# Two y buffers and two x buffers in place of one and three, and fewer unconditional rounds, in the expert stage of a hybrid encoder layer

## The chip, the cores and the metric

The kernel runs on one core of a Trainium2 chip. The metric is the device time of one execution in microseconds; three executions of the kernel before are given, and one of them was profiled.

## The reference, cut to what matters

One layer over 1024 prompt rows and 64 sample rows of width 1024: modulated RMSNorm, an input projection, two kinds of attention, an output projection, then a mixture of experts, and a last RMSNorm. The change touches only the mixture of experts:

```python
def hier_moe(h, w_rg, b_rg, w_re, b_re, w_gate, w_up, w_down):
    ...                                   # top-1 of 4 groups, top-2 of the 8 experts in it
    combine = jnp.einsum('tke,tk->te', jax.nn.one_hot(expert_id, N_EXPERTS, dtype=jnp.float32), e_w)

    def expert_step(acc, args):
        wg, wu, wd, cw = args
        hh = jax.nn.silu(x @ wg) * (x @ wu)
        return acc + (hh * cw[:, None].astype(hh.dtype)) @ wd, None
```

There are 32 experts with a hidden width of 256. Each of the 1088 rows goes to two of them, so 2176 pairs of row and expert are computed. All of it is in float32.

## The kernel before

Five stages follow one another: modulation and norm of the input, projection with attention (to about 690 us), output projection with routing (to about 920 us), the experts, and the last norm. The routing stage writes a list in HBM: for each expert the rows that chose it, where each result goes, and its weight. The expert stage is the function `experts` (line 1442).

The work is cut into blocks of 64 rows of one expert, and a step computes two blocks at once, block A in partitions 0 to 63 and block B in 64 to 127. For these inputs there are 26 steps, numbered p = 0 to 25 here, in 13 rounds of two. The number of rounds n is data: each engine reads it from a table, and the program is written out for 17 rounds (34 steps). `in_rounds` (line 1478) writes the loop out. The first `SURE` = 9 rounds are always needed and stand without a branch, the others behind `If(n > u)`. `following` (line 1491) does the same for work that belongs to a later step.

Weights come from HBM. Block A's expert is one of at most three held in slots (`a_gu`, `a_dn`), 3 MB loaded by SyncE when a slot comes free, 10 times in all. Block B's weights are loaded anew in each step by ScalarE's queue, `b_gu` (2 MB, three buffers, issued at line 1503 after the silu three steps ahead) and `b_dn` (1 MB, two buffers, line 1505, after the y eviction two steps ahead).

One step p goes through these places:

- POOL reads a piece of the list into `entry` (line 1545, `listing`), gathers 128 rows of `h2` by it into `x[p % 3]` (line 1550, `gather`), and at the end scatters the result rows `y` to HBM (line 1572). All three are indirect DMAs of POOL's one queue. Rows of padding in a block are skipped.
- PE transposes the gathered rows (line 1584), multiplies them by gate and up weights (lines 1595 and 1598: 16 pairs of matmul records a step), transposes the gated hidden rows (line 1605), and multiplies by the down weights (lines 1618 and 1621: 8 pairs).
- ACT and DVE each move a half of the transposed rows (1671, 1737), make the gated hidden rows (silu at 1677, product at 1741), move the transposed hidden rows (1749), and evict a half of the result, times the routing weight, into `y` (1695 and 1754).

The order within the engines is written out by hand. PE does in body p: gate and up of p+1, the hidden transposes of p, the row transposes of p+2, down of p. ACT does: load of gate and up weights for p+3, its half of the rows of p+2, its half of y of p, load of down weights for p+2, silu of p+1. POOL does: the gather for p+4 (once the row transposes of p+1 are done and their buffer is free), the scatter of p (once both halves of y are written), the list read for p+7. There is one buffer `y`, so both evictions of step p wait until the scatter of step p-1 has landed. Before the loop POOL has issued three list reads, three gathers, three list reads, a gather and a list read.

Of the kernel before, what the change touches and what calls it, by code (L numbers as in the profile page):

```python
# [18 lines left out]
F32 = mybir.dt.float32  # L19
F32R = mybir.dt.float32r  # L20
I32 = mybir.dt.int32
ALU = mybir.AluOpType
ACT = mybir.ActivationFunctionType
# [24 lines left out]
STEPS = 2 * ROUNDS  # L48
SURE = (2 * TOK // P + 1) // 2
LOOK = STEPS  # L50
# [91 lines left out]
def build(nc, a, o):  # L142
    with ExitStack() as ctx:
# [24 lines left out]
        with ExitStack() as c:  # L168
# [5 lines left out]
                done=route.sb("done", [P, 2, 2 * NE]), steps=route.sb("steps", [P, 1]), cols=route.sb("cols", [P, 8]),  # L174
                x=[route.sb(f"x{j}", [P, D]) for j in range(3)])
            with ExitStack() as c2:
# [843 lines left out]
def mix_out(nc, s, a, o, k, g2):  # L1020
# [112 lines left out]
    def _(pool):  # L1133
        pool.memset(half[:, :], -0.5).then_inc(half_set, 1)
        pool.memset(entry[:, :, :], 0).then_inc(zeroed, 1)
        pool.memset(before[:, :], 0.0).then_inc(zeroed, 1)
        for j in range(3):
            pool.memset(route["x"][j][:, :], 0.0).then_inc(x_zeroed, 1)
# [27 lines left out]
        pool.wait_ge(listed, 32 * (NT + 1))  # L1166
        pool.wait_ge(x_zeroed, 3)

# [273 lines left out]
def experts(nc, s, a, k):  # L1442
# [11 lines left out]
    hT = s.sb("hT", [P, 2, P])  # L1454
    y = s.sb("y", [P, D])
    rank, first, held = (s.sb(n, [P, 2 * NE]) for n in ("rank", "first", "held"))
# [7 lines left out]
    listed = [s.sem(f"listed{j}") for j in range(4)]  # L1464
    gathered, scattered = [s.sem(f"gathered{j}") for j in range(3)], s.sem("scattered")
    gu_ld, dn_ld = [s.sem(f"gu_ld{j}") for j in range(3)], [s.sem(f"dn_ld{j}") for j in range(2)]
# [12 lines left out]
    def in_rounds(eng, n, body):  # L1479
        for u in range(ROUNDS):  # L1480
            if u < SURE:
                body(2 * u, n)
                body(2 * u + 1, n)
            else:
                with eng.If(n > u):
                    body(2 * u, n)
                    body(2 * u + 1, n)
                with eng.Else():
                    eng.nop()

    def following(eng, p, n, do):

        if p // 2 < SURE:
            do()
        elif p < STEPS:
            with eng.If(n > p // 2):
                do()
            with eng.Else():
                eng.nop()
# [43 lines left out]
    def _(pool):  # L1543
# [4 lines left out]
        def gather(p):  # L1548
            pool.wait_ge(listed[p % 4], 16 * (p // 4 + 1))
            pool.indirect_dma_start(x[p % 3][:, :], None, k["h2"], bass.IndirectOffsetOnAxis(ap=entry[:, p, 0:1], axis=0),  # L1550
                                    bounds_check=TOK - 1, oob_is_err=False).then_inc(gathered[p % 3], 16)

        for p in range(3):
            listing(p)
        for p in range(3):
            gather(p)
        for p in range(3, 6):
            listing(p)
        n = look(pool, T_ROUNDS, 0, 1, ROUNDS)

        def gather_ahead(p):
            pool.wait_ge(xT_ready, p - 2)
            gather(p)

        gather_ahead(3)
        listing(6)

        def body(p, n):
            following(pool, p + 4, n, lambda: gather_ahead(p + 4))
            pool.wait_ge(y_out_act, p + 1)  # L1570
            pool.wait_ge(y_out_dve, p + 1)
            pool.indirect_dma_start(k["yrows"], bass.IndirectOffsetOnAxis(ap=entry[:, p, 1:2], axis=0), y[:, :], None,  # L1572
                                    bounds_check=2 * TOK - 1, oob_is_err=False).then_inc(scattered, 16)
            following(pool, p + 7, n, lambda: listing(p + 7))

        in_rounds(pool, n, body)
        alone(pool, scattered, 32 * n, waited)

    @block.tensor
    def _(pe):  # L1580
        def transpose_x(p):
            pe.wait_ge(gathered[p % 3], 16 * (p // 3 + 1))
            for c in range(NC):
                ins = pe.transpose(xT_ps[:, c, :], x[p % 3][:, c * P:(c + 1) * P], ident)
            ins.then_inc(xT_ready, 1)
# [49 lines left out]
        def body(p, n):  # L1635
# [4 lines left out]
            elif p + 1 < STEPS:  # L1640
                if p // 2 + 1 < SURE:
                    gate_up(p + 1)
                    transpose_hidden(p)
                    transpose_x(p + 2)
                else:
                    with pe.If(n > p // 2 + 1):
                        gate_up(p + 1)
                        transpose_hidden(p)
                        transpose_x(p + 2)
                    with pe.Else():  # L1650
                        transpose_hidden(p)
            else:
                transpose_hidden(p)
# [5 lines left out]
    def _(act):  # L1659
# [29 lines left out]
        def body(p, n):  # L1689
            following(act, p + 3, n, lambda: load_gu(p + 3, expert(p + 3)))  # L1690
            following(act, p + 2, n, lambda: move_xT(p + 2))
            act.wait_ge(y_ready, p + 1)
            if p:
                act.wait_ge(scattered, 16 * p)
            act.activation(y[:, 0:512], y_ps[:, 0:512], ACT.Copy, scale=entry[:, p, 2:3].bitcast(F32))\
               .then_inc(y_out_act, 1)
# [9 lines left out]
    def _(dve):  # L1706
# [40 lines left out]
        def body(p, n):  # L1747
# [3 lines left out]
            dve.wait_ge(y_ready, p + 1)  # L1751
            if p:
                dve.wait_ge(scattered, 16 * p)
            dve.tensor_scalar(y[:, 512:1024], y_ps[:, 512:1024], entry[:, p, 2:3].bitcast(F32), None, ALU.mult)\  # L1754
               .then_inc(y_out_dve, 1)
# [183 lines left out]
```

## Time and profile before

| | us |
|---|---|
| median of three executions | 1355.49 |
| lowest, highest | 1351.79, 1362.63 |
| the profiled execution | 1351.79 |
| its span, first to last instruction | 1349.6 |
| expert stage in it, about | 926 to 1294 |
| PE busy | 1161.5 (86%) |
| mean granted TensorE clock | 0.941 of full speed |

Times in rows are microseconds from the start of the span unless marked ns. An "issue" or a "q" behind an engine's name (PEldq, ACTq) is its instruction queue, PEld is TensorE's weight load. A wait is put down to what came last before the instruction started.

### The profile page before, as it was taken

To read this page: it belongs to the slowest core of one execution; us is meant where nothing else is said; L and a number is where in the kernel's file an instruction comes from. 1 tells how busy PE (TensorE), PEld (TensorE's weight loads), DVE (VectorE), ACT (ScalarE), POOL (GpSimd) and SP (SyncE) were. 2 spreads that over 40 slices of the span, in tenths; PEclk is the share of its full clock that TensorE was granted. 3 is DMA by queue.
4 is the path that set the end of the run, shared out by engine and by line. 5 is a ranking of instruction groups with operands and counts; after the bars stand their busy time and mean duration, and the time that the engine had idled before them with its cause. 6 is when DMAs were issued, how large, how long until landed. Compare 5 with 4: busy or idle time off the path is not lost. (4 is left out here: it accounts for less than half of the span.)

```text
span 1349.6 us, 19893 instructions
## 1 busy us (share of the span) xinstructions
PE 1161.5 (86%) x7175; PEld 767.0 (57%) x7175; DVE 518.6 (38%) x1320; ACT 342.2 (25%) x854; POOL 295.1 (22%) x233
## 2 busy tenths in 40 slices
PE   4688999999999999999886999951998999899846
PEld 2346888888888888888773555521333333333312
DVE  2432244444444444535533466653112121111118
ACT  4422233333332333333442222110101011111102
POOL 2031313030302121110002565533112221211001
PEclk9677999999999999999998999975999899999978
DMA  9771202020102121110130111115998999999646
GB/s 372 291 287 50 71 19 89 1 88 3 60 11 70 53 78 45 54 53 26 47 140 8 63 53 57 47 32 236 419 393 313 386 379 388 376 374 363 249 185 250
DMA packets 53538, 218.56 MB, mean 162 GB/s; under 512 B 9904, under 2 KB 26680, under 8 KB 42560
## 3 DMA queue, kind: packets, MB, share of 16 engines
q1 hardware_dynamic: 36912, 117.26, 23.7%
q10 hardware_dynamic: 7632, 82.05, 15.3%
q0 software_dynamic: 8896, 17.93, 3.4%
q8 instruction: 63, 1.03, 0.3%
q14 instruction: 35, 0.29, 0.1%
HBM read 196.62 MB, written 30.03 MB: 168 GB/s over the span
## 5 line engine op out<-in xcount | busy, mean ns | idle before, releaser
L729 PE MATMUL att_piece_ps<-hT_hi,w_hi 128*128 128x384 f32 (+1 forms) x528 | 185.2, 351 | 2.0 <-DVE att_k_lo_sb L857 0.8
L1595 PE MATMUL moe_gu_ps<-moe_a_gu_sb,moe_xT_sb 128*64 x416 | 184.4, 596 | 2.0 <-DVE moe_xT_sb L1737 2.0
L1598 PE MATMUL moe_gu_ps<-moe_b_gu_sb,moe_xT_sb 128*64 128x512 f32 x416 | 184.4, 596 | 0.0
L729 PE MATMUL att_piece_ps<-hT_hi,w_lo 128*128 128x384 f32 (+1 forms) x528 | 173.6, 329 | 0.0
L729 PE MATMUL att_piece_ps<-hT_lo,w_hi 128*128 128x384 f32 (+1 forms) x528 | 173.2, 328 | 0.0
L916 DVE COPY att_pT_sb<-att_pT_ps 128x512 f32<-128x512 f32 (+2 forms) x192 | 94.6, 521 | 134.0 <-PE att_pT_ps L790 133.4
L1200 PE MATMUL mix_y_ps<-mix_w_out_sb,mix_oT_sb 128*128 128x512 f32 (+1 forms) x288 | 127.2, 600 | 2.2 <-ACT mix_oT_sb L1268 2.2
L1595 PEld LDWEIGHTS moe_gu_ps<-moe_a_gu_sb,moe_xT_sb 128*64 128x64 f32 x416 | 57.2, 138 | 121.2 <-issue 121.2
L977 ACT ACTIVATE att_probs_sb<-att_probs_sb,att_nmax_sb 128x640 f32<-128x640 f32 (+5 forms) x144 | 101.2, 703 | 42.1 <-DVE att_nmax_sb L902 41.3
L902 DVE CUSTOM_DVE_ANT_0 att_probs_sb<-att_s_ps,att_bias_sb 128x640 f32<-128x640 f32 (+5 forms) x144 | 95.2, 662 | 26.8 <-PE att_s_ps L778 14.6
L729 PEld LDWEIGHTS att_piece_ps<-hT_hi,w_hi 128*128 128x128 f32 x528 | 99.8, 189 | 9.4 <-issue 4.7
L992 ACT ACTIVATE keep_rows_all_sb<-att_o_ps,att_rden_sb 128x64 f32<-128x64 f32 x144 | 37.2, 309 | 261.0 <-PE att_o_ps L811 261.0
L706 POOL CAST w_hi<-att_w_raw_sb 128x1024 fp32r<-128x1024 f32 x21 | 21.8, 1038 | 364.8 <-PE att_piece_ps L729 331.7
L1618 PE MATMUL moe_y_ps<-moe_a_dn_sb,moe_hT_sb 128*64 x208 | 99.2, 621 | 1.5 <-DVE moe_hT_sb L1749 0.7
L729 PEld LDWEIGHTS att_piece_ps<-hT_lo,w_hi 128*128 128x128 f32 x528 | 100.0, 189 | 0.0
L729 PEld LDWEIGHTS att_piece_ps<-hT_hi,w_lo 128*128 128x128 f32 x528 | 99.7, 189 | 0.0
L1621 PE MATMUL moe_y_ps<-moe_b_dn_sb,moe_hT_sb 128*64 128x512 f32 x208 | 99.2, 621 | 0.0
L1754 DVE TENSOR_SCALAR moe_y_sb<-moe_y_ps,moe_entries_sb 128x512 f32<-128x512 f32 x26 | 19.5, 751 | 204.2 <-DMA expert_rows<-moe_y_sb,moe_entries_sb 193.5
L1200 PEld LDWEIGHTS mix_y_ps<-mix_w_out_sb,mix_oT_sb 128*128 128x128 f32 (+1 forms) x288 | 52.9, 186 | 69.9 <-issue 67.0
L790 PE MATMUL att_pT_ps<-keep_consts_sb,att_probs_sb 128*128 128x128 f32 (+2 forms) x560 | 87.6, 278 | 1.8 <-ACT att_probs_sb L977 1.7
L1572 POOL DMA_INDIRECT expert_rows<-moe_y_sb,moe_entries_sb x26 | 26.2, 1010 | 254.0 <-DVE moe_y_sb L1754 254.0
L805 PE MATMUL att_o_ps<-att_pT_sb,att_v_rows_sb 128*64 128x128 f32 (+1 forms) x1088 | 74.4, 277 | 7.7 <-DVE att_pT_sb L916 6.5
(280 smaller groups left out, 1801.6 us busy)
## 6 DMA issues: line engine op xcount, KB each, us to landing
moe_b_gu_sb<-in_w_gu ACTq DMA_DIRECT2D x26, 2048.0 KB
moe_b_dn_sb<-in_w_dn ACTq DMA_DIRECT2D x26, 1024.0 KB
moe_a_gu_sb<-in_w_gu SPq DMA_DIRECT2D x10, 2048.0 KB
keep_rows_all_sb<-in_w_ada SPq DMA_DIRECT2D x8, 2048.0 KB, 12.2
att_w_raw_sb<-in_w_qkv SPq DMA_DIRECT2D x21, 512.0 KB, 3.3
moe_a_dn_sb<-in_w_dn SPq DMA_DIRECT2D x10, 1024.0 KB
in_w_ada_sb<-in_w_ada SPq DMA_DIRECT2D x4, 2048.0 KB, 11.5
in_x_sb<-in_x_prompt SPq DMA_DIRECT2D x8, 512.0 KB, 7.0
```

What stands on the lines that cost most here:

```text
L729: ins = pe.matmul(bank[:, 0:hi - lo], w[:, kind, kc, :], x[:, kc, lo:hi], start=(m == 0), stop=(m == 3 * NC - 1))
L790: ins = pe.transpose(pT_ps[e % 2][0:m, b - b0, 0:r], probs[h][0:r, b * P:b * P + m], ident[0:r, 0:r])
L805: ins = pe.matmul(o_ps[head, 0:r], v, pT[h][0:m, b, 0:r], start=(b == 0), stop=(b == len(kb) - 1))
L902: dve.tensor_tensor_reduce(probs[h][0:r, 0:wide], s_ps[h][0:r, 0:wide], bias, -SCALE, BIG, ALU.add, ALU.min, nmax[0:r, 2 * at + h:2 * at + ...
L916: ins = dve.tensor_copy(pT[h][:, b0:b1, :], pT_ps[e % 2][:, 0:b1 - b0, :])
L977: act.activation(probs[h][0:r, 0:wide], probs[h][0:r, 0:wide], ACT.Exp, bias=nmax[0:r, 2 * at + h:2 * at + h + 1], scale=-1.0, accum_out=d ...
L992: ins = act.activation(rows_all[0:r, t, first + HD * h:first + HD * h + HD], o_ps[0:r, P + HD * h:P + HD * h + HD], ACT.Copy, scale=rden[0 ...
L1200: ins = pe.matmul(y_ps[0:r, 512 * n:512 * n + 512], oT[:, c, 0:r], w_out[:, c, 512 * n:512 * n + 512], start=(c == 0), stop=(c == NC - 1))
L1595: pe.matmul(gu_ps[p % 2][LANE[0], :], xT[:, c, LANE[0]], a_gu[:, bass.ds(slot, 1), c, :].rearrange("p a n -> p (a n)"), start=(c == 0), st ...
L1598: ins = pe.matmul(gu_ps[p % 2][LANE[1], :], xT[:, c, LANE[1]], b_gu[p % 3][:, c, :], start=(c == 0), stop=(c == NC - 1))
L1618: pe.matmul(y_ps[LANE[0], half], hT[:, c, LANE[0]], a_dn[:, bass.ds(slot, 1), c, half].rearrange("p a n -> p (a n)"), start=(c == 0), stop ...
L1621: ins = pe.matmul(y_ps[LANE[1], half], hT[:, c, LANE[1]], b_dn[p % 2][:, c, half], start=(c == 0), stop=(c == 1))
```

## The change

It does three things, all for the expert stage.

1. `y` has two buffers, with a semaphore `scattered` for each. The evictions of step p wait for the scatter of step p-2.
2. The gathered rows `x` have two buffers in place of three. In body p POOL gathers for p+3. Before the loop it issues two list reads and two gathers, four more list reads, and then, once the first row transposes are done, the gather for step 2 and a seventh list read. The routing stage clears two x buffers in place of three. The bytes held in SBUF stay the same.
3. `SURE` is gone. Only round 0 is without a branch, in all engines; rounds 1 to 8 are now conditional as 9 and up were.

```diff
-SURE = (2 * TOK // P + 1) // 2
...
-                x=[route.sb(f"x{j}", [P, D]) for j in range(3)])
+                x=[route.sb(f"x{j}", [P, D]) for j in range(2)])
...
-        for j in range(3):
+        for j in range(2):
             pool.memset(route["x"][j][:, :], 0.0).then_inc(x_zeroed, 1)
...
-    y = s.sb("y", [P, D])
+    y = [s.sb(f"y{j}", [P, D]) for j in range(2)]
...
-    gathered, scattered = [s.sem(f"gathered{j}") for j in range(3)], s.sem("scattered")
+    gathered, scattered = ([s.sem(f"{n}{j}") for j in range(2)] for n in ("gathered", "scattered"))
...
     def in_rounds(eng, n, body):
         for u in range(ROUNDS):
-            if u < SURE:
-                body(2 * u, n)
-                body(2 * u + 1, n)
+            if u == 0:
+                body(0, n)
+                body(1, n)
...
     def following(eng, p, n, do):
-        if p // 2 < SURE:
+        if p // 2 == 0:
             do()
...
-        for p in range(3):
-            listing(p)
-        for p in range(3):
-            gather(p)
+        listing(0)
+        listing(1)
+        gather(0)
+        gather(1)
+        n = look(pool, T_ROUNDS, 0, 1, ROUNDS)
+        for p in range(2, 6):
+            following(pool, p, n, lambda: listing(p))
+
+        def third():
+            pool.wait_ge(xT_ready, 1)
+            gather(2)
+            following(pool, 6, n, lambda: listing(6))
+
+        following(pool, 2, n, third)
+
+        def gather_ahead(p):
+            pool.wait_ge(xT_ready, p - 1)
             gather(p)
-        for p in range(3, 6):
-            listing(p)
-        n = look(pool, T_ROUNDS, 0, 1, ROUNDS)
-
-        def gather_ahead(p):
-            pool.wait_ge(xT_ready, p - 2)
-            gather(p)
-
-        gather_ahead(3)
-        listing(6)
 
         def body(p, n):
-            following(pool, p + 4, n, lambda: gather_ahead(p + 4))
+            following(pool, p + 3, n, lambda: gather_ahead(p + 3))
             pool.wait_ge(y_out_act, p + 1)
             pool.wait_ge(y_out_dve, p + 1)
-            pool.indirect_dma_start(k["yrows"], bass.IndirectOffsetOnAxis(ap=entry[:, p, 1:2], axis=0), y[:, :], None,
-                                    bounds_check=2 * TOK - 1, oob_is_err=False).then_inc(scattered, 16)
+            pool.indirect_dma_start(k["yrows"], bass.IndirectOffsetOnAxis(ap=entry[:, p, 1:2], axis=0), y[p % 2][:, :], None,
+                                    bounds_check=2 * TOK - 1, oob_is_err=False).then_inc(scattered[p % 2], 16)
             following(pool, p + 7, n, lambda: listing(p + 7))
 
         in_rounds(pool, n, body)
-        alone(pool, scattered, 32 * n, waited)
+        alone(pool, scattered[0], 16 * n, waited)
+        alone(pool, scattered[1], 16 * n, waited)
...
-                if p // 2 + 1 < SURE:
+                with pe.If(n > p // 2 + 1):
                     gate_up(p + 1)
                     transpose_hidden(p)
                     transpose_x(p + 2)
-                else:
-                    with pe.If(n > p // 2 + 1):
-                        gate_up(p + 1)
-                        transpose_hidden(p)
-                        transpose_x(p + 2)
-                    with pe.Else():
-                        transpose_hidden(p)
+                with pe.Else():
+                    transpose_hidden(p)
...
             act.wait_ge(y_ready, p + 1)
-            if p:
-                act.wait_ge(scattered, 16 * p)
-            act.activation(y[:, 0:512], y_ps[:, 0:512], ACT.Copy, scale=entry[:, p, 2:3].bitcast(F32))\
+            if p >= 2:
+                act.wait_ge(scattered[p % 2], 16 * (p // 2))
+            act.activation(y[p % 2][:, 0:512], y_ps[:, 0:512], ACT.Copy, scale=entry[:, p, 2:3].bitcast(F32))\
                .then_inc(y_out_act, 1)
```

DVE's half of the eviction is changed as ACT's, and `gather` and `transpose_x` count their semaphores and buffers by two.

## Rows read from the trace of the kernel before

**Rows 1.** The page, part 2: busy tenths in 40 slices of 33.7 us.

```profile
PE   4688999999999999999886999951998999899846
...
DMA  9771202020102121110130111115998999999646
```

**Rows 2.** Windows: length, busy per engine, then clock, DMA share, GB/s.

```profile
950.00:962.00 12.00, 11.01 (x56) 4.13 (x54) 1.11 (x2) 0.98 (x2) 2.99 (x3) 1.00 1.01 420
...
926.00:1002.30 76.30, 55.42 (x262) 22.13 (x264) 10.07 (x23) 7.66 (x13) 16.03 (x16) 0.83 0.99 406
...
1002.30:1265.50 263.20, 241.87 (x1164) 91.55 (x1160) 45.77 (x80) 33.49 (x61) 56.69 (x57) 0.97 0.92 368
...
1265.50:1294.00 28.50, 19.88 (x94) 7.12 (x94) 5.48 (x10) 3.37 (x7) 3.83 (x4) 0.99 0.35 122
```

**Rows 3.** Waits, 920 to 1310: who waited for whom; total, times, longest us.

```profile
ACT moe_y_sb L1695 <- DMA expert_rows<-moe_y_sb,moe_entries_sb: 195.4, 23, 11.0
...
DVE moe_y_sb L1754 <- DMA expert_rows<-moe_y_sb,moe_entries_sb: 193.5, 23, 10.9
...
PE moe_hT_ps L1605 <- DVE moe_gate_sb L1741: 26.3, 17, 3.2
...
PE moe_xT_ps L1584 <- DMA route_x_sb<-h_rows,moe_entries_sb: 14.0, 1, 14.0
```

**Rows 4.** Tile moe_y_sb, 900 to 1310: the scatter, its time to landing.

```profile
DMA to landing us min/median/max: 3.2/11.4/17.9
```

**Rows 5.** Line 1545, 920 to 1310: the list reads, their time to landing.

```profile
DMA to landing us min/median/max: 5.9/10.8/18.5
```

**Rows 6.** Timeline of POOL: first gather; scatters of steps 2 and 22.

```profile
930.07 0.99 POOL L1550 DMA_INDIRECT route_x_sb<-h_rows,moe_entries_sb  x1 [3.00 <-DMA moe_entries_sb<-lists,route_at_sb]
...
1002.32 1.02 POOL L1572 DMA_INDIRECT expert_rows<-moe_y_sb,moe_entries_sb  x1 [9.43 <-DVE moe_y_sb L1754]
...
1265.45 0.99 POOL L1572 DMA_INDIRECT expert_rows<-moe_y_sb,moe_entries_sb  x1 [12.24 <-DVE moe_y_sb L1754]
```

**Rows 7.** Timeline, all engines, start of stage and two steady steps.

```profile
942.42 1.97 PE L1584 MATMUL moe_xT_ps<-keep_consts_sb,route_x_sb 128*128 128x128 f32 x8 [13.96 <-DMA route_x_sb<-h_rows,moe_entries_sb]
...
1121.27 0.69 ACT L1695 ACTIVATE moe_y_sb<-moe_y_ps,moe_entries_sb 128x512 f32<-128x512 f32 x1 [9.71 <-DMA expert_rows<-moe_y_sb,moe_entries_sb]
...
1122.90 1.02 POOL L1572 DMA_INDIRECT expert_rows<-moe_y_sb,moe_entries_sb  x1 [10.03 <-DVE moe_y_sb L1754]
...
1123.06 0.34 ACTq L1503 DMA_DIRECT2D moe_b_gu_sb<-in_w_gu  x1
...
1123.28 0.44 PE L1605 MATMUL moe_hT_ps<-keep_consts_sb,moe_gate_sb 128*128 128x128 f32 x2 [1.90 <-DVE moe_gate_sb L1741]
...
1124.52 0.64 PE L1618 MATMUL moe_y_ps<-moe_a_dn_sb,moe_hT_sb 128*64 x1
...
1125.55 0.99 POOL L1550 DMA_INDIRECT route_x_sb<-h_rows,moe_entries_sb  x1 [0.30 <-issue]
...
1128.01 0.59 PE L1595 MATMUL moe_gu_ps<-moe_a_gu_sb,moe_xT_sb 128*64 x1
...
1135.40 0.44 PE L1605 MATMUL moe_hT_ps<-keep_consts_sb,moe_gate_sb 128*128 128x128 f32 x2 [0.35 <-DVE moe_gate_sb L1741]
...
1136.64 0.64 PE L1618 MATMUL moe_y_ps<-moe_a_dn_sb,moe_hT_sb 128*64 x1
```

**Rows 8.** Lines 1496 and 1485: branches, ns; PE in a conditional round.

```profile
L1496 PEldq COMPARE_BRANCH  x9: 65/169/356, 1175.1 to 1273.5; - x9
...
L1485 PEldq COMPARE_BRANCH  x12: 65/169/5407, 1191.9 to 1295.1; - x12
...
1252.87 0.44 PE L1605 MATMUL moe_hT_ps<-keep_consts_sb,moe_gate_sb 128*128 128x128 f32 x2 [1.37 <-DVE moe_gate_sb L1741]
...
1254.21 0.64 PE L1618 MATMUL moe_y_ps<-moe_a_dn_sb,moe_hT_sb 128*64 x1
```

**Rows 9.** Line 1138: the memsets of the x buffers, ns.

```profile
L1138 POOL MEMSET route_x_sb<- x3: 967/967/967, 695.0 to 696.8; 128x1024 f32 x3
```

More of the change, by code:

```diff
@@ L1166, in _ @@
         pool.wait_ge(listed, 32 * (NT + 1))
-        pool.wait_ge(x_zeroed, 3)
+        pool.wait_ge(x_zeroed, 2)
     @block.tensor
@@ L1549, in gather @@
             pool.wait_ge(listed[p % 4], 16 * (p // 4 + 1))
-            pool.indirect_dma_start(x[p % 3][:, :], None, k["h2"], bass.IndirectOffsetOnAxis(ap=entry[:, p, 0:1], axis=0),
-                                    bounds_check=TOK - 1, oob_is_err=False).then_inc(gathered[p % 3], 16)
-        for p in range(3):
-            listing(p)
-        for p in range(3):
-            gather(p)
-        for p in range(3, 6):
-            listing(p)
-        n = look(pool, T_ROUNDS, 0, 1, ROUNDS)
-        def gather_ahead(p):
-            pool.wait_ge(xT_ready, p - 2)
-            gather(p)
-        gather_ahead(3)
-        listing(6)
+            pool.indirect_dma_start(x[p % 2][:, :], None, k["h2"], bass.IndirectOffsetOnAxis(ap=entry[:, p, 0:1], axis=0),
+                                    bounds_check=TOK - 1, oob_is_err=False).then_inc(gathered[p % 2], 16)
+        listing(0)
[12 more added lines that the diff above has]
+            pool.wait_ge(xT_ready, p - 1)
+            gather(p)
         def body(p, n):
-            following(pool, p + 4, n, lambda: gather_ahead(p + 4))
+            following(pool, p + 3, n, lambda: gather_ahead(p + 3))
             pool.wait_ge(y_out_act, p + 1)
             pool.wait_ge(y_out_dve, p + 1)
-            pool.indirect_dma_start(k["yrows"], bass.IndirectOffsetOnAxis(ap=entry[:, p, 1:2], axis=0), y[:, :], None,
-                                    bounds_check=2 * TOK - 1, oob_is_err=False).then_inc(scattered, 16)
+            pool.indirect_dma_start(k["yrows"], bass.IndirectOffsetOnAxis(ap=entry[:, p, 1:2], axis=0), y[p % 2][:, :], None,
+                                    bounds_check=2 * TOK - 1, oob_is_err=False).then_inc(scattered[p % 2], 16)
             following(pool, p + 7, n, lambda: listing(p + 7))
         in_rounds(pool, n, body)
-        alone(pool, scattered, 32 * n, waited)
+        alone(pool, scattered[0], 16 * n, waited)
+        alone(pool, scattered[1], 16 * n, waited)
     @block.tensor
@@ L1581, in transpose_x @@
         def transpose_x(p):
-            pe.wait_ge(gathered[p % 3], 16 * (p // 3 + 1))
+            pe.wait_ge(gathered[p % 2], 16 * (p // 2 + 1))
             for c in range(NC):
-                ins = pe.transpose(xT_ps[:, c, :], x[p % 3][:, c * P:(c + 1) * P], ident)
+                ins = pe.transpose(xT_ps[:, c, :], x[p % 2][:, c * P:(c + 1) * P], ident)
             ins.then_inc(xT_ready, 1)
@@ L1751, in body @@
             dve.wait_ge(y_ready, p + 1)
-            if p:
-                dve.wait_ge(scattered, 16 * p)
-            dve.tensor_scalar(y[:, 512:1024], y_ps[:, 512:1024], entry[:, p, 2:3].bitcast(F32), None, ALU.mult)\
+            if p >= 2:
+                dve.wait_ge(scattered[p % 2], 16 * (p // 2))
+            dve.tensor_scalar(y[p % 2][:, 512:1024], y_ps[:, 512:1024], entry[:, p, 2:3].bitcast(F32), None, ALU.mult)\
                .then_inc(y_out_dve, 1)
```

## The prediction

> **What bounds the kernel now.** I read four things in turn: the slices of the page, windows over the expert stage, the waits in it, and the timeline of two steps. The slices [rows 1] show where the change can act: PE is at 9 tenths nearly everywhere, and the DMA engines are busy only at the start and in slices 28 to 37, which are the expert stage (926 to 1294 us). Everything before 924 us is touched by one memset alone, so the whole sum is about this stage.
>
> The windows [rows 2] split it. From 926 to 1002 the DMA share is 0.99: three resident experts, the first streamed ones and the first rows all load at once, and steps 0 and 1 run in that. From 1002.3 to 1265.5 it is 0.92 at 368 GB/s with PE busy 241.87 of 263.2 us. The last 28.5 us have share 0.35. The middle window is chosen because the scatter of step 2 is issued at its start and that of step 22 at its end [rows 6]: (1265.45 - 1002.32) / 20 = 13.16 us a step. I call the length of a step T.
>
> The waits [rows 3] name a loop. ACT and DVE stand 195.4 and 193.5 us before their halves of the y eviction, 23 times, and what ends it is always the scatter of the step before, out of the same y buffer. Few of these microseconds are worth anything as such. PE's own stalls are what count: 26.3 us over 17 waits for the gated hidden rows (line 1741), which ACT and DVE can only make after the y eviction they are stuck in. PE waited for gathered rows once, at the very start (14.0 us), and never for weights: no weight tile stands among the releasers of its waits.
>
> The timeline [rows 7] shows one turn: y eviction 1121.27, the scatter issued 1122.90 (1.63 later), and it lands 11.4 us after its issue in the median [rows 4]. 1.63 + 11.4 = 13.0, the step of 13.16 almost exactly. So the middle stretch is bound by the round trip of the scatter.
>
> **Part one: two y buffers.** The eviction of step p now waits for scatter p-2. That allows 2T for a round trip of 13.0, so with T above 11 it is never last. The wait goes; three limits are next.
>
> PE itself: down starts are at 1124.52 and 1136.64, 12.12 apart, with 0.35 idle in between [rows 7], so a step of pure PE work is 11.77. Taken over the whole window it is 241.87 / 20 = 12.09 [rows 2], because the granted clock there was 0.97 of its upper level (2.4 GHz), with stretches at the lower one, and step starts don't overlap perfectly. T is at least 11.77 to 12.09.
>
> DMA: a share of 0.92 over 263.2 us is 242.1 us of work, 12.1 per step [rows 2]. Nothing in the change takes a byte away. T is at least 12.1, and that only with the DMA engines never idle. The window from 926 shows that 0.99 is possible when much is outstanding. Here the weights are fetched at most three steps ahead, each load released by the step's silu, so I take 0.97: 242.1 / 0.97 / 20 = 12.48, say 12.5. From both sides: 0.92 (nothing gained) gives 13.16, 1.0 gives 12.1.
>
> The Trainium skill, page "HBM Reference", section "Specifications (TRN2)", puts a core's effective share at about 358 GB/s and says that a core streaming alone measures about 425. By the first figure the stage, at 368, would be at its ceiling already and the sum would be zero; by the second there is room. The trace agrees with the second: 420 GB/s from 950 to 962 [rows 2].
>
> Loads that are released earlier: silu of step p no longer stands behind a late eviction, so the load of gate and up weights (issued at 1123.06, after silu [rows 7]) moves ahead relative to PE's work. That keeps the queue fuller and is why I dare 0.97. Gain of part one: 20 x (13.16 - 12.5) = 13.2 us.
>
> **Part two: two x buffers.** A gather is issued one step later: where POOL issued p+4 after the scatter of p-1 and a list read, it now issues p+3. The order on POOL is scatter, list read, gather, all in one queue; nothing else is queued behind them but the next scatter. The allowance: the y eviction of p-1 starts 3.6 us after its down (1124.52 to 1128.01 [rows 7], and 0.1 to start, an estimate), and the transposes of p+3 start 1.0 before the down of p+1 (the 1.24 us from 1123.28 to 1124.52 hold the two hidden transposes, then these), so it is 2T - 4.6. The gather is issued 1125.55 - 1121.27 = 4.3 after the eviction starts [rows 7]. It must land within 2T - 8.9 of its issue: 14.6 us at T = 11.77, 16.1 at T = 12.5.
>
> No view prints a gather's time to landing. From below: the scatter ahead of it in the queue lands 11.4 - 2.65 = 8.8 after the gather's issue, and a scatter alone takes 3.2 (the least of [rows 4]): 12.0. The first gather, with the DMA share at 0.99, took 942.42 - 930.07 = 12.4 [rows 6, 7]. From above: 18.5, the longest list read [rows 5], or 17.9, the longest scatter [rows 4]. I take 14 to 16, nearer the lower end where most rows are: just in time at T = 12.5. It costs nothing while PE has a step's work in hand; if that cover is gone, PE stands in the transposes (line 1584), the down product and the eviction behind them are late, and the loop gives T = (g + 8.9) / 2 for a mean landing g. It is worse than now only from g = 17.4 on.
>
> The start: the gather of step 2 moves from just after the second to behind the first transposes (end 944.4 [rows 7]). It has nearly two steps; late by at most 18.5 - 14.6 = 3.9 us, taken as 0, since the DMA engines are full there anyway and set the pace.
>
> **Part three: conditional rounds.** Rounds 1 to 8 (16 steps) now sit behind branches on PE, ACT, DVE and POOL, as rounds 9 to 12 do already. On PE such a branch took 0.17 us in the median [rows 8], issued ahead of its work. From hidden transposes to down it was 1.24 in an unconditional step [rows 7] and 1254.21 - 1252.87 = 1.34 in a conditional one [rows 8]: 0.1 x 16 = 1.6 us at most, 0 at least; I take 0.7.
>
> The Trainium skill, page "Runtime: NRT & Kernel Launch", section "Instruction fetch mechanics", says that a taken branch out of the two pages held makes the engine fetch before it goes on. By that rule each of the 8 rounds could stall; by the rows of the short jumps the part is worth the 0.7 just given.
>
> The memset that falls away (0.967 us of POOL at about 697 us [rows 9]) lies beside PE's work in the stage before and is worth 0 to 1; I take 0. The two waits at the end for the two scatter semaphores replace one, 0. Steps 0 to 2 and 23 to 25 gain nothing: the first are DMA bound (0.99), the last have a free queue (share 0.35) and PE does its chain.
>
> **The sum.** -13.2 + 0.7 = -12.5 us. The span of 1349.6 becomes 1337.1, the profiled execution's 1351.79 becomes 1339.3; the median of the three runs lies 3.7 above that execution, so 1355.5 - 12.5 = **1343.0**.
>
> **Rivals.**
> A, the full gain: T = 12.1, the bound of data and nearly that of PE. 20 x 1.06 = 21 us: 1334. For it: 0.99 has been reached, and clock dips vanish with the stalls (down to 11.77 by PE). Against: the loads are released by PE's own progress, and the three resident-expert loads come in bursts. The loosest edge, T = 11.77, would be 27.8 us, 1328.
> B, the gather takes the place: g about 16.9 while an expert load shares the engines, T = 12.9, gain 5, 1350. For it: landings of 17.9 and 18.5 occur [rows 4, 5]. Against: medians near 11.
> C, the other sign: PE waits in line 1584 for nearly every step. With g = 18.5, T = 13.7, +10.8; first gathers +3.9, branches +1.6: +16, 1371.5. It decides from a mean landing of 17.4. For it: the three transfers of a step stand in one queue, and with the engines fuller each takes longer. Against: a late gather also stops PE's releases of weight loads, and the queue clears.
> D, branches stall for a fetch: one branch of line 1485 took 5.407 us [rows 8], a far jump over the unused rounds. Eight such are +43: 1398. Against: all the near ones are of some 0.2 us. It is what the page "Runtime: NRT & Kernel Launch" of the Trainium skill would mean here.
> E, the data ceiling of 368 is real: no change, 1355. It is what the first figure of the page "HBM Reference" of the Trainium skill would mean here.
>
> **How the numbers follow.** Forecast (gain 8 to 17, 1338 to 1348) 0.40; A 0.17; B 0.24; C 0.13; D 0.03; E 0.03. One per cent, 13.6 us, is about what a measurement of this kernel can tell from nothing, and the forecast lies just inside it. Faster by over 1%: A and about half the forecast, 0.37. Within 1%: the other half, B, E, and the mild part of C, 0.49. Slower: 0.14. The range leaves out D, the worst half of C and the edge of A: 1330 to 1368; cases of both signs are in it.
>
> **What would show it.** Part one: the waits of lines 1695 and 1754 on the scatter gone, those on line 1621 in their place; PE's wait at line 1605 near 0. The data limit: DMA share near 0.97 between the scatters of steps 2 and 22, these 250 us apart. Part two: waits of line 1584 on the gather few and short; over 10 us in total is B, over 30 is C. Part three: no idle time of PE at round starts. The forecast is wrong if scatters still come 13 us apart with the share at 0.92, or closer than 12.

## The result

The changed kernel takes 1370.57 us in the median of eight executions (1362.44 to 1373.47) against 1357.45 of the kernel before on the same chip (1351.79 to 1362.63): a ratio of 1.0084, with a 95% interval of 1.0060 to 1.0108. It is slower by 11 us by the ratio, and by 13 by the two medians. The range of 1330 to 1368 did not hold it, and a gain had been forecast. A second set on another chip gave 1.0081 (1.0052 to 1.0110).

The profiled execution has a span of 1368.6 us against 1349.6. Where most of the 19 us are, the same windows show: length, then busy time with instruction count of PE, PE's weight load, DVE, ACT and POOL, then granted clock, DMA share and GB/s. The second one runs from the scatter of step 2 to that of step 22, as the window of before did.

```profile
926.00:1002.30 76.30, 53.69 (x254) 21.45 (x256) 12.10 (x34) 7.86 (x13) 18.64 (x19) 0.82 0.98 401
...
999.70:1279.30 279.60, 250.19 (x1164) 96.90 (x1162) 45.77 (x80) 33.41 (x61) 57.69 (x58) 0.94 0.88 351
```

Up to 1002 us nothing has changed much: share 0.98 for 0.99, PE busy 53.69 for 55.42 [rows 2]. Between the two scatters there are now 279.6 us in place of 263.1, a step of 13.98 for 13.16, and the DMA share is 0.88 where it was 0.92. That is 16.4 of the 19 us; the scatter of step 2 comes 2.6 us earlier than before, and what follows the scatter of step 22 takes 5.2 longer (1368.6 - 1279.3 against 1349.6 - 1265.5). The DMA engines, which were to be the new bound, stand idle more than before. PE's busy time has grown from 241.87 to 250.19 us for the same 1164 instructions, and its clock has gone from 0.97 to 0.94.

The waits from 920 to 1320 us (engine and line, what it waited for, total, times, longest), where [rows 3] showed the scatter:

```profile
PE moe_xT_ps L1588 <- DMA route_x_sb<-h_rows,moe_entries_sb: 45.8, 10, 14.0
...
ACT moe_y_sb L1694 <- PE moe_y_ps L1625: 99.0, 26, 9.8
...
PE moe_hT_ps L1609 <- DVE moe_gate_sb L1740: 1.5, 1, 1.5
```

The scatter no longer stands among what ACT waits for; it waits for the down product of PE, as it should. The stall of 26.3 us at the hidden rows is down to 1.5. In their place PE waits 45.8 us for gathered rows, ten times and not once. Without the first, 14.0 us long as before, that is 31.8 us: above the 30 at which the prediction had said "C".

The timeline of POOL, start and length first, shows the two scatters that give the step (1279.26 - 999.70, over 20), and one gather in between:

```profile
999.70 1.02 POOL L1575 DMA_INDIRECT expert_rows<-moe_y_sb,moe_entries_sb  x1 [8.88 <-DVE moe_y_sb L1753]
...
1055.23 0.99 POOL L1549 DMA_INDIRECT route_x_sb<-h_rows,moe_entries_sb  x1 [0.30 <-issue]
...
1279.26 1.01 POOL L1575 DMA_INDIRECT expert_rows<-moe_y_sb,moe_entries_sb  x1 [14.96 <-DVE moe_y_sb L1753]
```

### The profile page after: what moved, and what is told of

The parts are those of the page before. It is cut to its first block and busy times, and to the rows that moved or that the text cites. A ratio compares the mean times of both kernels' runs of the same rounds, so it can differ in the third digit from the quotient of the medians.

```text
span 1368.6 us, 20186 instructions
## 1 busy us (share of the span) xinstructions
PE 1169.7 (85%) x7175; PEld 772.9 (56%) x7175; DVE 519.8 (38%) x1320; ACT 342.2 (25%) x854; POOL 294.5 (22%) x232
## 5 line engine op out<-in xcount | busy, mean ns | idle before, releaser
L1199 PE MATMUL mix_y_ps<-mix_w_out_sb,mix_oT_sb 128*128 128x512 f32 (+1 forms) x288 | 130.3, 612 | 2.2 <-ACT mix_oT_sb L1267 2.2
L1622 PE MATMUL moe_y_ps<-moe_a_dn_sb,moe_hT_sb 128*64 x208 | 106.0, 657 | 1.8 <-issue 1.0
L1625 PE MATMUL moe_y_ps<-moe_b_dn_sb,moe_hT_sb 128*64 128x512 f32 x208 | 106.1, 658 | 0.0
L1575 POOL DMA_INDIRECT expert_rows<-moe_y_sb,moe_entries_sb x26 | 26.3, 1011 | 270.8 <-DVE moe_y_sb L1753 270.8
L1588 PE MATMUL moe_xT_ps<-keep_consts_sb,route_x_sb 128*128 128x128 f32 x208 | 33.2, 312 | 45.8 <-DMA route_x_sb<-h_rows,moe_entries_sb 45.8
## 6 DMA issues: line engine op xcount, KB each, us to landing
keep_rows_all_sb<-in_w_ada SPq DMA_DIRECT2D x8, 2048.0 KB, 12.1
moe_a_dn_sb<-in_w_dn SPq DMA_DIRECT2D x10, 1024.0 KB, 19.8
```

Of the source, the lines that this page charges most:

```text
L1199: ins = pe.matmul(y_ps[0:r, 512 * n:512 * n + 512], oT[:, c, 0:r], w_out[:, c, 512 * n:512 * n + 512], start=(c == 0), stop=(c == NC - 1))
L1622: pe.matmul(y_ps[LANE[0], half], hT[:, c, LANE[0]], a_dn[:, bass.ds(slot, 1), c, half].rearrange("p a n -> p (a n)"), start=(c == 0), stop ...
L1625: ins = pe.matmul(y_ps[LANE[1], half], hT[:, c, LANE[1]], b_dn[p % 2][:, c, half], start=(c == 0), stop=(c == 1))
```

## When the gather is late

The timelines of SyncE and PE of the changed kernel. The first three lines are SyncE issuing resident expert loads of 2 MB (the next line of code adds 1 MB), the others are PE, with the wait in front of an instruction in brackets:

```profile
998.86 0.34 SPq L1502 DMA_DIRECT2D moe_a_gu_sb<-in_w_gu  x1
...
1051.74 0.34 SPq L1502 DMA_DIRECT2D moe_a_gu_sb<-in_w_gu  x1
...
1249.41 0.34 SPq L1502 DMA_DIRECT2D moe_a_gu_sb<-in_w_gu  x1
...
1021.08 1.14 PE L1588 MATMUL moe_xT_ps<-keep_consts_sb,route_x_sb 128*128 128x128 f32 x8 [4.12 <-DMA route_x_sb<-h_rows,moe_entries_sb]
...
1074.26 1.97 PE L1588 MATMUL moe_xT_ps<-keep_consts_sb,route_x_sb 128*128 128x128 f32 x8 [4.42 <-DMA route_x_sb<-h_rows,moe_entries_sb]
...
1076.16 1.12 PE L1622 MATMUL moe_y_ps<-moe_a_dn_sb,moe_hT_sb 128*64 x1
...
1088.78 1.04 PE L1588 MATMUL moe_xT_ps<-keep_consts_sb,route_x_sb 128*128 128x128 f32 x8
...
1271.43 1.97 PE L1588 MATMUL moe_xT_ps<-keep_consts_sb,route_x_sb 128*128 128x128 f32 x8 [3.92 <-DMA route_x_sb<-h_rows,moe_entries_sb]
```

Seven expert loads are issued after the start, and seven gathers are late by 3.8 to 4.5 us, one for each. PE starts on them some 22 us after the load's issue (1021.08 - 998.86 = 22.2, 1074.26 - 1051.74 = 22.5, 1271.43 - 1249.41 = 22.0). The gather issued at 1055.23, 3.5 us after a load, is the one that PE has in hand at 1074.26: 19.0 us, of which PE stood the last 4.42, so 14.6 was what it could have had for nothing. Of the other gathers after step 5, none is waited for at all.

The landing times of all 26 gathers, least, median and longest, by the view of the tile `route_x_sb`, which has them for the changed kernel:

```profile
DMA to landing us min/median/max: 8.8/14.9/19.8
```

So there is more than one group, and after step 5 it goes by the load: a gather away from a load lands in some 9 to 11 us, the late one in 18.4 to 19.8, and the one behind it in 14 to 16. This last one costs nothing, since the late step before it has stretched its own allowance to over 20 us. The median of 14.9 lies in the 14 to 16 that were forecast; what costs time are the seven above it.

The wait is not all that it costs. After 4.42 us of standing PE transposes the eight pieces in 1.97 us, where the next step takes 1.04, and the first down products take 1.12 instead of 0.59 to 0.64. Windows of PE right behind the wait and a little later, same columns as above:

```profile
1074.20:1079.50 5.30, 5.24 (x16) 2.58 (x18) 0.69 (x1) 0.60 (x1) 0.00 (x0) 0.50 0.83 347
...
1083.00:1088.00 5.00, 5.00 (x26) 1.54 (x22) 0.42 (x1) 0.38 (x1) 3.04 (x3) 1.00 0.91 305
```

The granted clock is 0.50 (the lower level of 1.2 GHz) from 1074.2 to 1079.5, after the engine had stood, and 1.00 (2.4 GHz) again from 1083. The Trainium skill, page "TensorE: Matmul & The Clock Gate", section "HAM oscillation — how this bites in real kernels", describes the same course, waits for DMA that put the engine back to 1.2 GHz, and prices it at half of the time spent there. The clock of 0.94 over the 279.6 us between the two scatters means that about 12% of them, 33.6 us, were spent at the lower level; by that price they cost 16.8 us, an estimate; the measured excess is 16.3 (below). The stretch shown is one of the longer ones: after the wait of 4.12 us at 1021.08 the transposes still took 1.14 us, and the lower level was over by 1026.

The length of a wait alone does not tell whether the clock falls. In the kernel before, two waits for the gated hidden rows, and the windows of PE behind each:

```profile
1030.00 0.44 PE L1605 MATMUL moe_hT_ps<-keep_consts_sb,moe_gate_sb 128*128 128x128 f32 x2 [1.98 <-DVE moe_gate_sb L1741]
...
1030.50:1033.80 3.30, 3.30 (x14) 1.74 (x14) 1.09 (x2) 0.60 (x1) 2.15 (x3) 0.50 1.04 402
...
1175.14 0.44 PE L1605 MATMUL moe_hT_ps<-keep_consts_sb,moe_gate_sb 128*128 128x128 f32 x2 [2.89 <-DVE moe_gate_sb L1741]
...
1175.20:1180.00 4.80, 4.74 (x27) 2.26 (x29) 1.12 (x2) 0.60 (x1) 2.60 (x3) 1.00 1.00 378
```

After 1.98 us of standing the clock was 0.50, after 2.89 us it stayed at 1.00. All seven waits of 3.8 to 4.5 us in the changed kernel were followed by the lower level.

The parts add up. A run without any such wait (e5 below) needs 233.9 us between the two scatters, PE busy in all of it. The changed kernel needs 279.6: 45.7 more. Seven waits are 29.1 of them, and PE's busy time is 250.19 - 233.90 = 16.3 longer, which goes with the clock of 0.94 against 1.00. Together 45.4.

## The experiments

Times are compared with the kernel before on the same chip. Theory L is that the late gathers are the cause. In e1 to e4 the three parts of the change are taken one by one, and then the gather alone is moved.

**e1: part two alone, two x buffers.** The reads and gathers ahead of the loop are also ordered as in the changed kernel.

```diff
 (kernel before)
-    x=[route.sb(f"x{j}", [P, D]) for j in range(3)]
+    x=[route.sb(f"x{j}", [P, D]) for j in range(2)]
...
-    following(pool, p + 4, n, lambda: gather_ahead(p + 4))
+    following(pool, p + 3, n, lambda: gather_ahead(p + 3))
```

> The kernel before with part two alone: two x buffers and POOL's gathers one step later; one y buffer and nine unconditional rounds stay. Theory L (late gathers: in the changed kernel only the gathers that share the engines with an expert load land late, 19 us after issue against an allowance near 14.6, and each such wait also drops the TensorE clock): PE waits for gathered rows in many steps, here more than in the changed kernel because the late y eviction shortens the allowance, over 40 us in all, and the time is 1370 to 1390. Rival Y (the second y buffer is to blame: it fills the queues) and rival B (the branches are): 1353 to 1361, with PE's only gather wait the first.

Measured: 1360.89 us, ratio 1.0001 (0.9976 to 1.0026). Its waits:

```profile
PE moe_xT_ps L1588 <- DMA route_x_sb<-h_rows,moe_entries_sb: 42.4, 9, 14.1
...
PE moe_hT_ps L1609 <- DVE moe_gate_sb L1745: 1.7, 2, 1.5
...
ACT moe_y_sb L1699 <- DMA expert_rows<-moe_y_sb,moe_entries_sb: 92.6, 17, 7.7
```

The late gathers are there, 28.3 us of waits after the first, but the time is not what L expected: it lies in the 1353 to 1361 of rivals Y and B, whose other sign, no gather wait but the first, did not come. The wait at the hidden rows, 26.3 us before, is down to 1.7, and the one at the gather, about as long, has come in its place. My expectation had added the two. That both come from the same slow stretches of POOL's queue, so that a step pays once, is how I read it; no run shows it. A later repetition beside the changed kernel is e11.

**e2: part three alone, the branches.**

```diff
 (kernel before)
-SURE = (2 * TOK // P + 1) // 2
+SURE = 1
```

> The kernel before with part three alone: rounds 1 to 8 conditional. Theory L: 0 to +2 us, 1355 to 1360. Rival B: at least +8 us, 1365 or more, and idle time of PE at the starts of rounds 1 to 8.

Measured: 1362.57 us, ratio 1.0008 (0.9984 to 1.0032). No measurable cost; rival B is out as the main cause here. The branches of the rounds in the changed kernel (name, shortest, median and longest in ns):

```profile
L1484 PEldq COMPARE_BRANCH  x28: 65/169/3527, 982.2 to 1314.8; - x28
```

0.169 us in the median, as in [rows 8], now in 28 places. The longest, 3.527 us, would be the far jump over the unused rounds, as the prediction read the 5.407 of [rows 8].

**e3: part one alone, two y buffers beside three x buffers.** There is no room for the fifth buffer, so the gate rows of the last stage are kept for one condition, with wrong values and the same work but for ACT, which copies half as much of them ahead of the expert stage. That stage starts at the same time (first resident load at 924.5 us, before 924.0).

```diff
 (kernel before)
-    y = s.sb("y", [P, D])
+    y = [s.sb(f"y{j}", [P, D]) for j in range(2)]
...
-    "gate2_rows", [P, 2, D]
+    "gate2_rows", [P, 1, D]
```

> The kernel before with part one alone: two y buffers with three x buffers. The room for the fifth buffer comes from the routing stage's gate rows, which are kept for one condition in place of two; so the last stage's gate is wrong in its values, the work is the same. Theory L: without the late gathers the gain that was forecast for part one appears: step 12.1 to 12.5 us, time 1336 to 1347, PE's only gather wait the first. Rival Y: 1357 or more, since the second y buffer costs what it brings.

Measured: 1332.62 us, ratio 0.9783 (0.9752 to 0.9815). This is the gain that the prediction had hoped for and twice its size, and below the expected 1336 to 1347. Waits, and the time to landing of its scatters (least, median, longest):

```profile
PE moe_xT_ps L1589 <- DMA route_x_sb<-h_rows,moe_entries_sb: 19.1, 2, 14.0
...
ACT moe_y_sb L1700 <- DMA expert_rows<-moe_y_sb,moe_entries_sb: 10.1, 2, 6.4
...
DMA to landing us min/median/max: 3.2/18.2/25.3
```

One late gather (5.0 us) is left beside the first one. The scatters now take 18.2 us in the median for 11.4 [rows 4], and twice they still hold the eviction up, which two buffers were thought to exclude. The gathers are slower too, 21.7 us in the median and 31.3 at most, but with three x buffers PE takes one up some 26 us after its issue, so only one of them was late. That landings grow with what stands in the queue and on the engines fits this; no run separates the two.

**e4: the changed kernel with the gather moved ahead of the eviction.** Nothing else differs from the changed kernel.

```diff
 (changed kernel)
         def body(p, n):
-            following(pool, p + 3, n, lambda: gather_ahead(p + 3))
+            following(pool, p + 4, n, lambda: gather_ahead(p + 4))
             pool.wait_ge(y_out_act, p + 1)
...
+        following(pool, 3, n, lambda: gather_ahead(3))
         in_rounds(pool, n, body)
```

In body p the transposes of p+2 come before the down product of p, so x is free for p+4 already then. POOL had gone to wait for the eviction first and issued this gather one body later, behind the scatter and the list read.

> The changed kernel with one thing moved: POOL issues the gather for p+4 before it waits for the y eviction of p, once the row transposes of p+2 are done, and so ahead of the scatter and the list read in its queue. Allowance from issue becomes two steps less 1 us, 22 us. Theory L: no gather is late, step 11.8 to 12.5 us, time 1334 to 1347. Rivals Y and B: as the changed kernel, 1365 to 1375, since nothing of theirs is touched.

Measured: 1332.63 us, ratio 0.9798 (0.9758 to 0.9839), 28 us below the kernel before by the medians, and faster than both. Its waits, and the window from the scatter of step 2 to that of step 22:

```profile
PE moe_xT_ps L1589 <- DMA route_x_sb<-h_rows,moe_entries_sb: 19.2, 3, 14.2
...
ACT moe_y_sb L1695 <- DMA expert_rows<-moe_y_sb,moe_entries_sb: 3.1, 1, 3.1
...
998.80:1239.90 241.10, 236.38 (x1164) 90.52 (x1162) 45.76 (x80) 33.36 (x61) 56.76 (x56) 0.99 0.99 401
```

Gather waits are down to 19.2 us with the first in them, the step is 241.1 / 20 = 12.06, and the DMA share is 0.99. One gather was still late, by 2.8 us, where the expectation had none, although the allowance had grown to 21.6 us. With the same two x buffers, two y buffers and branches, the sign of the whole change turns by where one DMA is issued.

**e5: the changed kernel with light expert loads.** After the first three, a resident load fetches 64 columns of one chunk, so block A computes in part with an older expert's weights.

```diff
 (changed kernel)
-            weights(sp, ex, a_gu[:, r, :, :], a_dn[:, r, :, :], slot_ld[r], slot_ld[r])
+            if m < SLOTS:
+                weights(sp, ex, a_gu[:, r, :, :], a_dn[:, r, :, :], slot_ld[r], slot_ld[r])
+            else:
+                sp.dma_start(a_gu[:, r, 0:1, 0:64], ...).then_inc(slot_ld[r], 16)
+                sp.dma_start(a_dn[:, r, 0:1, 0:64], ...).then_inc(slot_ld[r], 16)
```

> The changed kernel, but the resident expert loads after the first three fetch only 64 columns of the first chunk in place of 3 MB each (the weights of block A are then partly those of an older expert, so its results are wrong in value; PE's work is the same). Theory L: the seven late gathers were late because such a load shared the engines; now no gather is later than 14.6 us, PE's waits for gathered rows after step 2 are gone, step 11.7, the stage ends about 42 us earlier than in the changed kernel: 1322 to 1335. Rival Q (the gather is late by its place behind scatter and list read, whatever else the engines do): waits of some 30 us stay, 1355 or more.

Measured: 1324.56 us, ratio 0.9742 (0.9686 to 0.9797).

```profile
PE moe_xT_ps L1592 <- DMA route_x_sb<-h_rows,moe_entries_sb: 16.2, 3, 14.0
...
996.40:1230.30 233.90, 233.90 (x1164) 90.01 (x1162) 45.77 (x80) 33.40 (x61) 57.65 (x57) 1.00 0.88 328
```

All gather waits after step 4 are gone with POOL's order as in the changed kernel; from step 6 on no gather took over 11.1 us to land. PE is busy 233.90 of 233.9 us, 11.70 a step. So the queue place alone does not make a gather late (rival Q falls): it takes the place and an expert load on the same engines. The run also has seven times 3 MB less to move in all; that the load beside the gather counts, and not the smaller total, is read from the timeline of the changed kernel, with one late gather behind each load.

**e6: the gather moved by its place in the queue only.** POOL still waits for the eviction first.

```diff
 (changed kernel)
         def body(p, n):
-            following(pool, p + 3, n, lambda: gather_ahead(p + 3))
             pool.wait_ge(y_out_act, p + 1)
             pool.wait_ge(y_out_dve, p + 1)
+            following(pool, p + 4, n, lambda: gather_ahead(p + 4))
             pool.indirect_dma_start(k["yrows"], ...)
```

> The changed kernel with only the place in the queue moved: POOL still waits for the y eviction of p, but then issues the gather (for p+4, the same buffer turn as the changed kernel's p+3 one body on) before the scatter and the list read and not behind them. The gather is issued 2.65 us earlier and has nothing of its step ahead of it. Theory L with place: landing from issue 6 to 14 us against an allowance of 17, so waits for gathered rows after step 2 are under 5 us: 1332 to 1345. Rival E (what e4 gained came from issuing 8 us earlier, before the eviction): some 20 us of waits stay, 1355 to 1368.

Measured: 1342.32 us, ratio 0.9881 (0.9826 to 0.9936).

```profile
PE moe_xT_ps L1589 <- DMA route_x_sb<-h_rows,moe_entries_sb: 24.4, 4, 14.2
...
ACT moe_y_sb L1695 <- DMA expert_rows<-moe_y_sb,moe_entries_sb: 10.7, 2, 5.9
```

10.2 us of gather waits after the first, of them 8.2 after step 2, in place of 31.8 and 29.5 in the changed kernel; the expectation of under 5 was too good. The profiled execution, 1333.38 us, is also the fastest of the five by 8 us, so the others probably waited longer. Five of the seven gathers that are issued within 1.0 us behind a load landed in 13.4 to 14.9 us, where the changed kernel's took 18.4 to 19.8; the other two took 20.8 and 21.5 and were late against an allowance of 17.1. So to have no scatter and list read ahead in the queue brings the larger part of the gain of e4, with the 2.5 us of longer allowance; issuing before the eviction brings more, by the medians (1342 and 1333, on two chips), but the two intervals touch.

**e7: the kernel before, a second profile.**

> The kernel before once more, for a second profile. The profiled execution of before was at the low edge of its runs. Expected: the stage from the first gate product to the last down product 340 to 348 us (339.7 in the first), scatter waits of ACT near 195 us, PE's wait for the gated rows near 26.

Measured: 1363.9 us in its one execution. From the start of the first gate product to that of the last down product it is 1299.67 - 947.83 = 351.8 us, and in the first profile 1288.19 - 945.38 = 342.8; the 339.7 of the expectation is not what the trace gives, and 351.8 lies over its 340 to 348.

```profile
ACT moe_y_sb L1695 <- DMA expert_rows<-moe_y_sb,moe_entries_sb: 202.4, 22, 11.9
...
PE moe_hT_ps L1605 <- DVE moe_gate_sb L1741: 31.6, 20, 4.2
```

202.4 and 31.6 us for 195.4 and 26.3 [rows 3]: the first profile lay at the low edge of the runs, so gains are larger against the medians than against that profile, and the loss of the changed kernel smaller. Between the scatters of steps 2 and 22 this profile has 268.3 us, a step of 13.42, and the changed kernel 11.3 more.

**e8: e4 with nine unconditional rounds.** The edit puts `SURE` back in `in_rounds`, `following` and PE's body.

> e4_gather_first with nine unconditional rounds again: the version that should beat both kernels. Theory L: as e4 within 0.3 per cent, 1328 to 1336, since the branches cost nothing that can be measured. Rival B: 5 us or more better than e4.

Measured: 1333.48 us, ratio 0.9802 (0.9761 to 0.9843). The same as e4; again no price of the branches.

**e9, e10, e11: the changed kernel, the same without its branches, and two x buffers alone, on one chip.** e10 is the changed kernel with `SURE` back, e11 is e1 again.

> The changed kernel once more, beside the next three on one chip, to tell what its parts add to each other. Theory L: its late gathers alone set it, and the second y buffer brings nothing while they do; so it stands within 0.5 per cent of e11 (two x buffers alone) and of e10 (the change without its branches): 1363 to 1372. Rival Y2 (the second y buffer costs something beside two x buffers): 6 us or more above e11.

> The changed kernel with nine unconditional rounds again (parts one and two of the change, not part three). Theory L: within 0.3 per cent of the changed kernel. Rival B (branches matter where POOL is late, as its list reads and gathers before the loop and in each body stand behind them): 5 us or more faster than it.

> e1_x2_only again, on the same chip as e9. Theory L: within 0.5 per cent of e9, and 0 to 5 us from the kernel before: its late gathers take the place of the scatter's wait, since both come from the same POOL queue during an expert load. Rival Y2: 6 us or more below e9.

Measured: e9 1371.23 us, 1.0081 (1.0052 to 1.0110); e10 1367.89 us, 1.0052 (1.0031 to 1.0074); e11 1366.11 us, 1.0044 (1.0016 to 1.0072). The gather waits of e11:

```profile
PE moe_xT_ps L1588 <- DMA route_x_sb<-h_rows,moe_entries_sb: 37.2, 9, 14.0
```

Two x buffers alone cost 0.44% here and nothing in e1; the second y buffer beside them adds nothing that the intervals show (e10 against e11), and the branches 3 us by the medians (e9 against e10), with intervals that overlap. So part two takes away the whole 2.2% that the second y buffer brings beside three x buffers (e3). What the other two parts add to the loss is at most a few microseconds each and is not settled. e9 lies 5.1 us above e11, inside L's 0.5 per cent (6.8 us) and under rival Y2's 6, but not far from it. e11 lies 5.7 us above the kernel before, where 0 to 5 was expected.

**e12: the kernel before with the gather first.**

```diff
 (kernel before)
-            following(pool, p + 4, n, lambda: gather_ahead(p + 4))
+            following(pool, p + 5, n, lambda: gather_ahead(p + 5))
...
         listing(6)
+        gather_ahead(4)
```

> The kernel before (one y buffer, three x buffers) with e4's order alone: the gather for p+5 is issued before POOL waits for the y eviction of p, ahead of the scatter. Theory L: no gain, 1355 to 1375, since the scatter's round trip is what binds here, and it now stands behind a gather that was issued some microseconds ahead of it. Rival O (the order alone was the gain of e4): 1330 to 1345.

Measured: 1363.43 us, ratio 1.0028 (1.0008 to 1.0049).

```profile
ACT moe_y_sb L1696 <- DMA expert_rows<-moe_y_sb,moe_entries_sb: 205.9, 23, 13.7
...
PE moe_xT_ps L1585 <- DMA route_x_sb<-h_rows,moe_entries_sb: 14.3, 1, 14.3
```

The order alone gains nothing. With one y buffer the scatter's round trip binds (205.9 us of waits), wherever the gather stands. With two x buffers both are needed: two y buffers so that the scatter may be late, and the gather in front since it may not. With three x buffers the second y buffer is enough (e3).

## Why the prediction was wrong

**What bound the kernel: right.** The loop of eviction and scatter was the bound: with it gone and few waits in its place the step fell from 13.16 to 12.06 (e4) and 12.28 (e3, 245.6 us over 20 steps).

**Part one's limits: right for PE, too slow for the data.** PE's own step was put at 11.77 and is 11.70 (e5). The data limit was put at 12.1, and e4's mean step of 12.06 with share 0.99 looks like it, but is not: the first ten of those twenty steps took 117.1 us, 11.71 each, at 409 GB/s with PE busy in all of it, below the limit of 12.1:

```profile
998.80:1115.90 117.10, 117.10 (x584) 45.62 (x582) 22.88 (x40) 16.73 (x31) 30.43 (x31) 1.00 1.00 409
```

I had dared 0.97 as the share; 0.99 was reached over the twenty. Of the two figures in the Trainium skill, page "HBM Reference", section "Specifications (TRN2)", the traces bear out the second: e4 moved 401 GB/s over 241 us, above 358 and below 425. "It is never last" was a little too strong: two evictions in e3 still waited for scatters of up to 25.3 us, since the landing time of 11.4 had been taken over from the kernel before, and grew to 18.2 here.

**Part two: the step that failed.** The prediction worked out the allowance rightly (14.6 us at a step of 11.77; PE stood from 14.6 us after the issue on). Its value for the landing was right as well: 14 to 16, and the median was 14.9. The step that failed is the next one, which put this one value, as the mean, into T = (g + 8.9) / 2 and called it free. A ring of two buffers does not work on the mean. A gather that lands at 10 gives nothing back to the next one, and one that lands at 19 costs the whole excess over 14.6, that is 4.4 us: what PE's waits show, 3.8 to 4.5. Seven of them are 29.1 us. The upper bound of 18.5 was also passed, by the longest of 19.8. The rows to see it by were there: 26 gathers, 10 expert loads and landing times from 3.2 to 18.5 in [rows 4, 5] say that slow ones come; what makes them slow, the expert load, was named in rival B, but priced as a mean of 16.9 for a gain of 5.

**The clock was left out of the price of a stall.** After each of these seven waits PE went on at the lower level for some microseconds, 5.3 after the one shown: 16.3 us in total, more than half as much again as the waits. The prediction had seen 0.97 in [rows 2] and counted on its rise (rival A), and not on its fall.

**Part three: right.** 0 to 1.6 us was the range, e2 gives 1.0008 of 1361, about 1 us, with 3.3 us either way; e9 against e10 leaves 3 us open. The rule in the Trainium skill, page "Runtime: NRT & Kernel Launch", section "Instruction fetch mechanics", has its case, if anywhere, in the one long branch of 3.527 us. Rival D is out.

**Which rival it was.** C, in its mechanism and place (line 1584, now 1588) and with 31.8 us of waits over its mark of 30. Its size was put at +16 and is +13 by the medians (1370.57 - 1357.45). But it was priced as nearly every step late with a mean landing of 18.5, while it is seven steps in 26, each with its clock. That the size came close is luck: it was reached by another sum. For that reason its deciding point, a mean landing of 17.4, was too high, and so its chance of 0.13 too low.

## What to carry to other kernels

When a buffer is taken from one ring and given to another, compare each ring's allowance with the slowest landing that recurs, not with the mean: only the excess of the late ones counts, and early ones repay nothing. Where several transfers of a step share one queue, issue first the one with the least slack (here the gather before the scatter), as soon as its buffer is free: this alone turned +0.8% into -2.0%. And add the clock to the price of a PE stall: seven waits of about 4 us cost half of their length again here.

## What the runs showed of the hardware that was not expected

The scatters of one kernel took 11.4 us to land in the median and those of another 18.2 (e3), with the same bytes; the least was 3.2 in both. The gathers went from 14.9 (changed kernel) to 21.7 (e3). So the same transfers took longer to land in the faster kernel. TensorE ran at a granted clock of 0.50 for 5.3 us after a wait of 4.4 us, with full speed before; among shorter waits one of 1.98 us was followed by 0.50 and one of 2.89 us was not. Two x buffers alone gave 1.0001 on one chip and 1.0044 on another, with intervals of 0.25 and 0.28% either way that overlap a little.
